# Second mixer of a two-block transformer: the recurrence's jobs, the head norms and the rotations are issued between groups of the input projection's products; the final norm becomes one DVE pass

## The chip, the cores and the metric

The kernel runs on one core of a Trainium2 chip. A core has five engines with a queue each: TensorE (PE, with its weight loads shown apart as PEld), VectorE (DVE), ScalarE (ACT), GpSimd (POOL) and SyncE (SP, which issues most DMAs). They meet only through semaphores: an engine works off its queue in order, and an instruction that waits holds everything behind it on that engine. The metric is the time of one execution of the whole program in microseconds.

## The reference, cut to what matters

A first block (two layers) makes x of 512 tokens by 1024 features. The second block is where the change is:

```python
hx = modulate(rmsnorm(x, g_norm1[l]), mx[0], mx[1])          # 512 tokens
hc = modulate(rmsnorm(ctx, g_norm1[l]), mc[0], mc[1])        # 256 context tokens
px = jnp.split(hx @ w_in[l], IN_SPLIT_IDX, axis=-1)
pc = jnp.split(hc @ w_in[l], IN_SPLIT_IDX, axis=-1)
qx = apply_rope(rmsnorm(heads(px[0], ATT_HEADS, ATT_HEAD_DIM), g_q[l]), cos, sin)
kx = apply_rope(rmsnorm(heads(px[1], ATT_KV_HEADS, ATT_HEAD_DIM), g_k[l]), cos, sin)
att_x = latent_attention(qx, kx, vx, kc, vc)
hg_x, hg_c = hgrn2_bidirectional(px[3:], pc[3:], lb_all[l], g_hg[l])
x = x + mx[2] * (jnp.concatenate([att_x, hg_x], axis=-1) @ w_out[l])
x = x + mx[5] * swiglu(...)
return rmsnorm(x, g_final)
```

`hgrn2_bidirectional` is a gated linear recurrence, four heads of 128 features, forward and backward: `fg = lb + (1 - lb) * sigmoid(f)`, the keys are `1 - fg`, the decays are `exp` of sums of `log(fg)`, and `o_t = S_t^T q_t` with `S_t = diag(fg_t) S_(t-1) + k_t v_t^T`. Its output is normed per head and multiplied by `silu(g)`.

## The kernel before, in words

Everything is kept feature-major: a tile is 128 features by 512 tokens (T) or 256 context tokens (LC). A float32 product is made of three cheaper ones: a chunk of 128 output features of a weight is loaded (`w_raw`, 4 slots), ACT copies its high half (`w_hi`, L160), DVE subtracts (`w_lo`, L166), both with 2 slots, and PE runs `w_hi*xH`, `w_hi*xL`, `w_lo*xH` for each of 8 groups of input features (L196): 24 products a chunk. Stages (`Stage` with `first_high`, `finished`, `emptied`, `high`, `low`) chain such projections.

The second mixer has four parts in a row, each a program of its own for the five queues:

1. `ProjectBoth` (L1802 to L1840): 26 chunks of `w_in`. The first 12 (attention queries, recurrence queries `hq`, output gates `hg`) multiply x alone; 14 (keys, values, `i`, forget gates `ff` and `fb`) also the 256 context columns. ACT copies each result out of its bank (L1830, L1831).
2. Head norms and rotations (L2016 to L2166): squares, means by a matrix product, `Ln` and `Exp`, rotation; six tiles. The sigmoids of all forget gates (L2024) stand here, and POOL prepares gates and keys (L2009 to L2013).
3. The attention loop, u = 0 to 31 and its tail: logits, softmax, turned probabilities, values. At u = 8 ACT takes the logarithms of all gates (`gate_logs`, L2042), and from u = 14 on DVE sums them (scans, L1923 and L1925).
4. The recurrence (L2256 to L2515). A unit u is a head and a direction (8 units). Within a block of 128 tokens the decayed products of queries and keys are made on 7 levels of halving, so there are 56 jobs n. A job is: two differences on DVE (L2415, L2416), one `Exp` on ACT (L2353), two multiplications on POOL (L2293, L2294), four products of 128x128 on PE, each of two weight loads (L2502), and a masked copy on DVE (L2404). Once a unit the decayed keys are turned (L2444, L2446), copied by ACT (L2321, L2322) and multiplied into state sums (L2455, L2458); once a head there are the diagonal (L2468), the output (L2480, L2483), its mean and its readout (L2328 to L2394).

After it the `Residual` stage begins the projection `w_out` (PE at 1854.28). At the very end the final `Norm` runs on DVE (L1289), then POOL (L1309), then SP stores (L1418).

## Time and profile before

| | us |
|---|---|
| median of 3 runs (2299.24 to 2299.47) | 2299.24 |
| the profiled execution | 2297.08 |
| its span | 2295.5 |
| PE busy in the span | 2122.0 (92%) |
| DVE busy | 1245.0 (54%) |
| ACT busy | 876.3 (38%) |
| POOL busy | 334.8 (15%) |

The mean granted TensorE clock is 0.958 of full speed. Busy times are sums over engines that run at once, so they don't add up to the span. Of the second mixer the projection ends at 1541.0, the norms and rotations at 1568.8, the attention at 1688.0, and the first product of `w_out` starts at 1854.28. Lines such as L2502 are lines of the kernel before, unless they are said to be of the changed kernel.

### The profile page before, as it was taken

The page shows a single profiled execution, that of the slowest core. Times are in us where ns is not written, and L with a number is a line of the kernel's source. Part 1 is how long each engine was busy: PE and PEld are TensorE (multiplying, and loading weights), DVE is VectorE, ACT ScalarE, POOL GpSimd, SP SyncE. Part 2 cuts the span into 40 slices and gives each one's busy share as a digit, 9 for nine tenths or more (in the row PEclk, how much of TensorE's full clock was granted, in tenths as well). Part 3 has the DMA queues.
Part 4 walks back from the last instruction along what each step waited for, and adds up shares of the span by engine and source line. Part 5 has one row for each costly group of instructions (what it writes and reads, how often), then busy time and mean ns, then how long its engine had stood idle before and what let it go on. Part 6 is the DMA issues. An engine that isn't in the chain of part 4 may idle for free. (4 is left out here: it accounts for less than half of the span.)

```text
span 2295.5 us, 27519 instructions
## 1 busy us (share of the span) xinstructions
PE 2122.0 (92%) x9734; PEld 1678.5 (73%) x9734; DVE 1245.0 (54%) x1922; ACT 876.3 (38%) x1345; POOL 334.8 (15%) x412
## 2 busy tenths in 40 slices
PE   8999879999999899899999979997877788999996
PEld 6666547888888677688888848884656667888885
DVE  3666437788667655766653352116749934333323
ACT  4433534444422443444442242227554524222222
POOL 0033312010000210100000030004039802000001
PEclk9999899999999999999999989997988889999998
DMA  5211002566445222132332212210000022333330
GB/s 190 76 44 37 1 29 67 183 197 193 151 156 157 95 83 83 56 101 92 100 116 96 81 37 92 64 46 1 1 10 10 13 79 66 101 91 101 110 101 37
DMA packets 52624, 191.78 MB, mean 84 GB/s; under 512 B 5792, under 2 KB 8512, under 8 KB 52288
## 3 DMA queue, kind: packets, MB, share of 16 engines
q1 hardware_dynamic: 44672, 163.07, 22.2%
q0 software_dynamic: 7344, 27.27, 3.8%
q8 instruction: 47, 0.77, 0.1%
q10 hardware_dynamic: 528, 0.40, 0.1%
q14 instruction: 33, 0.27, 0.0%
HBM read 187.05 MB, written 3.67 MB: 83 GB/s over the span
## 5 line engine op out<-in xcount | busy, mean ns | idle before, releaser
L196 PE MATMUL psum<-xH,w_hi 128*128 128x512 f32 x1800 | 719.0, 399 | 48.2 <-DVE xL L1297 23.5
L196 PE MATMUL psum<-xL,w_hi 128*128 128x512 f32 x1800 | 707.9, 393 | 0.0
L196 PE MATMUL psum<-xH,w_lo 128*128 128x512 f32 x1800 | 707.6, 393 | 0.0
L166 DVE TENSOR_TENSOR w_lo<-w_raw,w_hi 128x1024 fp32r<-128x1024 f32 (+1 forms) x273 | 353.4, 1295 | 443.9 <-ACT w_hi L160 443.9
L160 ACT ACTIVATE w_hi<-w_raw 128x1024 fp32r<-128x1024 f32 (+1 forms) x273 | 303.1, 1111 | 398.6 <-PE psum L196 394.1
L196 PEld LDWEIGHTS psum<-xH,w_hi 128*128 128x128 f32 x1800 | 342.0, 190 | 147.9 <-DVE xL L1297 38.4
L196 PEld LDWEIGHTS psum<-xH,w_lo 128*128 128x128 f32 x1800 | 342.1, 190 | 72.8
L196 PEld LDWEIGHTS psum<-xL,w_hi 128*128 128x128 f32 x1800 | 342.8, 190 | 67.9 <-issue 0.5
L196 PE MATMUL psum<-hidH,w_hi 128*128 128x512 f32 x528 | 206.2, 391 | 0.0
L196 PE MATMUL psum<-hidH,w_lo 128*128 128x512 f32 x528 | 205.4, 389 | 0.0
L196 PE MATMUL psum<-hidL,w_hi 128*128 128x512 f32 x528 | 205.4, 389 | 0.0
L1375 DVE SCALAR_TENSOR_TENSOR gate_value<-psum,cols,gate_value 128x511 f32<-128x511 f32 x88 | 66.0, 750 | 133.5 <-ACT gate_value L1348 132.5
L1348 ACT ACTIVATE gate_value<-psum,cols 128x512 f32<-128x512 f32 x88 | 60.7, 689 | 164.0 <-PE psum L196 164.0
L1311 POOL TENSOR_SCALAR xT<-y,cols 128x512 f32<-128x512 f32 x32 | 40.1, 1262 | 554.8 <-DVE y L1289 554.8
L196 PEld LDWEIGHTS psum<-hidH,w_hi 128*128 128x128 f32 x528 | 99.1, 188 | 21.1 <-issue 0.5
L196 PEld LDWEIGHTS psum<-hidL,w_hi 128*128 128x128 f32 x528 | 99.1, 188 | 21.0 <-issue 0.5
L196 PEld LDWEIGHTS psum<-hidH,w_lo 128*128 128x128 f32 x528 | 99.1, 188 | 20.5
L2502 PE MATMUL psum<-gla_mixed 128*128 128x128 f32 x448 | 70.7, 310 | 33.6 <-POOL gla_mixed L2294 30.7
L2502 PEld LDWEIGHTS psum<-gla_mixed 128*128 128x128 f32 x448 | 61.8, 214 | 43.1 <-POOL gla_mixed L2294 40.7
L612 ACT ACTIVATE logits<-logits,stat 128x128 f32<-128x128 f32 (+3 forms) x64 | 36.0, 562 | 107.2 <-DVE stat L740 107.1
L740 DVE CUSTOM_DVE_ANT_0 logits<-psum,addend 128x128 f32<-128x128 f32 (+3 forms) x64 | 31.3, 490 | 82.6 <-PE psum L846 80.4
L1378 DVE SCALAR_TENSOR_TENSOR gate_value<-psum,cols,gate_value 128x510 f32<-128x510 f32 x88 | 65.9, 748 | 11.1 <-DVE gate_value L1375 2.8
(312 smaller groups left out, 2538.0 us busy)
## 6 DMA issues: line engine op xcount, KB each, us to landing
w_raw<-in_up SPq DMA_DIRECT2D x132, 512.0 KB, 3.5
w_raw<-in_down SPq DMA_DIRECT2D x48, 704.0 KB, 4.0
mod_raw<-in_mod POOLq DMA_DIRECT2D x48, 512.0 KB, 3.8
w_raw<-in_sb_in SPq DMA_DIRECT2D x26, 512.0 KB, 3.5
w_raw<-in_ev_in SPq DMA_DIRECT2D x23, 512.0 KB, 3.6
w_raw<-in_od_in SPq DMA_DIRECT2D x20, 512.0 KB, 3.5
w_raw<-in_ev_out SPq DMA_DIRECT2D x8, 512.0 KB, 3.5
w_raw<-in_od_out SPq DMA_DIRECT2D x8, 512.0 KB, 3.4
```

Of the source, the lines that this page charges most:

```text
L160: nc.scalar.activation(w_hi[:, s % SPLIT, 0:w.cols], raw[:, s, 0:w.cols], ACT.Copy).then_inc(w.high, 1)
L166: nc.vector.tensor_tensor(w_lo[:, s % SPLIT, 0:w.cols], raw[:, s, 0:w.cols], w_hi[:, s % SPLIT, 0:w.cols].bitcast(F32), ALU.subtract).then ...
L196: mm = nc.tensor.matmul(acc, a[:, slot % SPLIT, cut], b[:, k0 + k, :], start=start and n == 0, stop=stop and n == 2)
L612: nc.scalar.activation(t, t, ACT.Exp, bias=stat[:, 0, s:s + 1], scale=-1.0, accum_out=stat[:, 1, s:s + 1]).then_inc(a["exp"], 1)
L740: nc.vector.tensor_tensor_reduce(out=tl[:, s % RING, 0:n], in0=logits_bank(s)[:, 0:n], in1=Xa[:, s % 3, 0:n], scale=-1.0 if kind == "a" el ...
L1311: ins = nc.gpsimd.tensor_scalar(dst, yt[:, t % 3, 0:self.n], self.gain(t), self.shift(t), ALU.mult, ALU.add)
L1348: nc.scalar.activation(value if j % 2 else gate, bank[j % 2][:, :], ACT.Copy, scale=self.tap(i, j, 2)).then_inc(ff["tap"], 1)
L1375: nc.vector.scalar_tensor_tensor(y[:, 1:T], acc[:, 0:T - 1], self.tap(i, j, 1), y[:, 1:T], ALU.mult, ALU.add).then_inc(ff["conv"], 1)
L1378: self.emptied(nc.vector.scalar_tensor_tensor(y[:, 2:T], acc[:, 0:T - 2], self.tap(i, j, 0), y[:, 2:T], ALU.mult, ALU.add), j)
L2502: mm = nc.tensor.matmul(bank[n % 3][:, blk(c)], x[:, blk(c)], x[:, blk(c)], start=True, stop=True)
```

## The change

`ProjectBoth`, the head norms, the attention and the recurrence become one stage, `SecondMixer`. The chunks of `w_in` come in a new order, `SB_LIST`: forget gates and `i` head by head, then keys, values, queries and output gates. From the third chunk on the products are cut into 76 `PARTS` of 12 products: two parts of 512 columns, and for a chunk with context two of 256 columns. After part p PE does job p - 14 of the recurrence, DVE and ACT do their share of job p - 11 at their own part p; POOL goes job by job. `sigmoid`, POOL's `gates`, `gate_logs` and `sum_gates` are done for one head at a time, between jobs. All turned tiles of the recurrence use one bank (5), each turn waiting until the one before has been copied out (`turned_out`). The context products use bank 2 alone. Head means and rotations run at p = 61 to 71. The attention loop keeps ten steps of the recurrence's readout. The first two chunks are not interrupted. The final norm is one `scalar_tensor_tensor` on DVE, in place, and the stores wait for it.

```diff
+                        if self.kind == "final":
+                            y = self.x[:, t, :]
+                            nc.vector.scalar_tensor_tensor(y, y, self.gain(t), rstd[:, :], ALU.mult, ALU.mult).then_inc(nm["y"], 1)
+                            continue
...
+                if self.kind == "final":
+                    return
...
-                    sp.wait_ge(nm["affine"], self.norm.at("affine", t))
-                    sp.dma_start(out[:, t, :], ht[:, t % 3, :]).then_inc(s_out[t % 3], 16)
-                for s in range(3):
-                    sp.wait_ge(s_out[s], 16 * len(range(s, KD, 3)))
+                    sp.wait_ge(nm["y"], self.norm.at("y", t))
+                    sp.dma_start(out[:, t, :], self.norm.x[:, t, :]).then_inc(s_out, 16)
+                sp.wait_ge(s_out, 16 * KD)
```

The order of the chunks, the parts and the offsets:

```diff
+        SB_LIST = [("hq", 0), ("hq", 1), ("ff", 0), ("fb", 0), ("i", 0), ("ff", 1), ("fb", 1), ("i", 1),
+                   ("hq", 2), ("ff", 2), ("fb", 2), ("i", 2), ("hq", 3), ("ff", 3), ("fb", 3), ("i", 3),
+                   ("k", 0), ("v", 0), *(("q", m) for m in range(4)), *(("hg", m) for m in range(HG))]
+        PLACE = {"hq": SB_HQ, "ff": SB_FF, "fb": SB_FB, "i": SB_I, "k": SB_K, "v": SB_V, "q": SB_Q, "hg": SB_HG}
+        W["sb_in"].order = tuple(PLACE[name] + m for name, m in SB_LIST)
...
+        PARTS, FIRST = [], {}
+        for c, (name, _) in enumerate(SB_LIST):
+            FIRST[c] = len(PARTS)
+            if c >= SPLIT:
+                PARTS += [(c, False, 0), (c, False, 4)] + ([(c, True, 0), (c, True, 4)] if name in C_TILE else [])
+        ENDED = {FIRST[c + 1] if c + 1 < SB_N else len(PARTS): c for c in range(1, SB_N)}
...
+        AHEAD = 11
+        PE_AT = 14
```

POOL (gates of one head, decayed keys, the loop) and ACT (results, sigmoids, logarithms, the keys' copy, the loop):

```diff
+                def gates(hd):
+                    pool.wait_ge(g["sig"], 4 * hd + 5)
+                    for d in range(2):
+                        u, t = 2 * hd + d, d * HG + hd
                         for f in (bx(u), bc(u)):
                             nc.gpsimd.tensor_scalar(f, f, lbs[:, 5, t:t + 1], lbs[:, 0, t:t + 1], ALU.mult, ALU.add)\
                                 .then_inc(g["fg"], 1)
...
+                def to_end(u):
+                    pool.wait_ge(g["to_end"], u + 1)
+                    x0 = (u % 2) * P
+                    nc.gpsimd.tensor_tensor(kds[:, 0:3 * P], kds[:, 0:3 * P], kx[:, u % 4, x0:x0 + 3 * P], ALU.mult)
+                    nc.gpsimd.tensor_tensor(kds[:, 3 * P:5 * P], kds[:, 3 * P:5 * P], kc[u % 4][:, :], ALU.mult).then_inc(g["kd"], 1)
...
+                gates(0)
+                for n in range(JOBS):
+                    u, l = n // LEVELS, n % LEVELS
+                    pool.wait_ge(g["exp"], n + 1)
+                    if n >= 3:
+                        pool.wait_ge(g["level"], n - 2)
+                    eq, ek, _ = halves(dec[:, n % 4, :], u, l)
+                    mq, mk, _ = halves(mixed[:, n % 3, :], u, l)
+                    nc.gpsimd.tensor_tensor(mq, halves(hq(u // 2), u, l)[0], eq, ALU.mult)
+                    nc.gpsimd.tensor_tensor(mk, halves(kx[:, u % 4, :], u, l)[1], ek, ALU.mult).then_inc(g["mult"], 1)
+                    if l == 2:
+                        to_end(u)
+                    hd = due(n, 9, 2 * LEVELS, HG - 1)
+                    if hd is not None:
+                        gates(hd + 1)
...
+                def result(c):
+                    name, m = SB_LIST[c]
+                    self.finished(act, 0, c)
+                    if c in CTX_DONE:
+                        nc.scalar.activation(sb_hc[:, C_TILE[name](m), :], bank[2][:, 0:LC], ACT.Copy).then_inc(ctx_out, 1)
+                    if name == "hg":
+                        act.wait_ge(g["mult"], JOBS)
+                    self.emptied(nc.scalar.activation(sb_hT[:, X_TILE[name](m), :], bank[c % 2][:, :],
+                                                      ACT.Silu if c < SPLIT else ACT.Copy), c)
+                    self.high(act, 0, c, c + SPLIT < w.n)
+
+                def sigmoid(hd):
...
+                    for u in (2 * hd, 2 * hd + 1):
+                        for f in (bx(u), bc(u)):
+                            nc.scalar.activation(f, f, ACT.Sigmoid).then_inc(g["sig"], 1)
+
+                def gate_logs(hd):
+                    act.wait_ge(g["k"], 4 * hd + 4)
+                    for u in (2 * hd, 2 * hd + 1):
+                        for f in (bx(u), bc(u)):
+                            nc.scalar.activation(f, f, ACT.Ln).then_inc(g["ln"], 1)
...
+                def kd_out(u, half):
+                    act.wait_ge(g["turned"], kd_turn_no(u, half))
+                    if half == 0 and u:
+                        act.wait_ge(g["kv"], u)
+                    dst = kd_tm[:, 0:3, :] if half == 0 else kd_tm[:, 3:5, :]
+                    src = bank[5][:, 0:(3 - half) * P].rearrange("t (c k) -> t c k", c=3 - half)
+                    nc.scalar.activation(dst, src, ACT.Copy).then_inc(g["turned_out"], 1)
...
+                def decays(n):
+                    if 0 <= n < JOBS:
+                        act.wait_ge(g["diff"], n + 1)
+                        d = dec[:, n % 4, :]
+                        nc.scalar.activation(d, d, ACT.Exp).then_inc(g["exp"], 1)
...
+                result(0)
+                for p in range(len(PARTS)):
+                    if p in ENDED:
+                        result(ENDED[p])
+                    hd = due(p, 20, 14, HG - 1)
+                    if p == 8 or hd is not None:
+                        sigmoid(0 if p == 8 else hd + 1)
+                    hd = due(p, 23, 14, HG - 1)
+                    if p == 11 or hd is not None:
+                        gate_logs(0 if p == 11 else hd + 1)
+                    decays(p - AHEAD)
```

DVE and PE:

```diff
+                def sum_gates(hd):
+                    dve.wait_ge(g["ln"], 4 * hd + 4)
+                    dve.wait_ge(g["inside"], 2)
+                    for u in (2 * hd, 2 * hd + 1):
+                        turn = slice(None, None, 1 if u % 2 == 0 else -1)
+                        nc.vector.tensor_tensor_scan(bx(u)[:, turn], inside[:, :], bx(u)[:, turn], 0.0, ALU.mult, ALU.add)\
+                            .then_inc(g["scan"], 1)
+                        nc.vector.tensor_tensor_scan(bc(u)[:, turn], bc(u)[:, turn], bc(u)[:, turn], 0.0, ALU.add, ALU.bypass)\
+                            .then_inc(g["scan"], 1)
...
+                def difference(n):
+                    u, l = n // LEVELS, n % LEVELS
...
+                    nc.vector.tensor_tensor(dq, q, border, ALU.subtract)
+                    nc.vector.tensor_tensor(dk, border, k, ALU.subtract).then_inc(g["diff"], 1)
...
+                def gla(n):
+                    hd = due(n, -1, 2 * LEVELS, HG)
+                    if hd is not None:
+                        sum_gates(hd)
+                    if 0 <= n < JOBS:
+                        difference(n)
+                    u = due(n, 10, LEVELS, U7)
+                    if u is not None:
+                        states(u)
+                    if 3 <= n < JOBS + 3:
+                        select(n - 3)
...
+                def part(c, ctx, k0):
+                    if k0 == 0 and not ctx:
+                        pe.wait_ge(acc_free[c % 2], self.free_at(0, c))
+                        pe.wait_ge(w.low, w.c0 + c + 1)
+                    elif k0 == 0 and CTX_DONE[c] > 1:
+                        pe.wait_ge(ctx_out, CTX_DONE[c] - 1)
+                    right = (cH, cL) if ctx else self.right
+                    acc = bank[2][:, 0:LC] if ctx else bank[c % 2][:, :]
+                    for k in range(k0, k0 + 4):
+                        mm = product(pe, w, c, right, acc, k, 0, k == 0, k == KD - 1)
+                    if k0 and (ctx or c not in CTX_DONE):
+                        mm.then_inc(w.used, 1)
+
+                def level(n):
+                    pe.wait_ge(g["mult"], n + 1)
+                    if n >= 2:
+                        pe.wait_ge(g["pred"], n - 1)
+                    x = mixed[:, n % 3, :]
+                    for c in range(NB):
+                        mm = nc.tensor.matmul(bank[3 + n % 2][:, blk(c)], x[:, blk(c)], x[:, blk(c)], start=True, stop=True)
+                    mm.then_inc(g["level"], 1)
...
+                def turn_keys(u, half):
+                    pe.wait_ge(g["kd"], u + 1)
+                    pe.wait_ge(g["turned_out"], kd_turn_no(u, half) - 1)
+                    for c in range(3 - half):
+                        mm = nc.tensor.transpose(bank[5][:, blk(c)], kds[:, blk(3 * half + c)], ident[:, :])
+                    mm.then_inc(g["turned"], 1)
...
+                def gla(n):
+                    if 0 <= n < JOBS:
+                        level(n)
+                        u, l = n // LEVELS, n % LEVELS
+                        if l < 2 and u % 2 == 0:
+                            turn_values(u // 2, l)
+                        if l in (2, 3):
+                            turn_keys(u, l - 2)
+                        if l == 5:
+                            sums(u)
...
+                for p, (c, ctx, k0) in enumerate(PARTS):
+                    part(c, ctx, k0)
+                    gla(p - PE_AT)
```

The order of instructions, first on PE in the recurrence. Before, the level products of consecutive jobs (L2502) stand directly behind one another, with the key turns (L2444, L2446) between them:

```order
L2502 MATMUL psum<-gla_mixed 128x128 [waits gla_pred,gla_mult]
L2502 MATMUL psum<-gla_mixed 128x128 x3
L2444 MATMUL psum<-ident,sb_hT 128x128 [waits gla_kd_out,gla_kd]
L2444 MATMUL psum<-ident,sb_hT 128x128 x2
L2446 MATMUL psum<-ident,sb_hT 128x128 x2
L2502 MATMUL psum<-gla_mixed 128x128 [waits gla_pred,gla_mult]
```

After, at the part that ends in job 10 (unit 1, the second half of its key turn; L2432 is the level product and L2449 the key turn of the changed kernel, L196 a product of the projection):

```order
L196 MATMUL psum<-xH,w_lo 128x512
L2432 MATMUL psum<-gla_mixed 128x128 [waits gla_pred,gla_mult]
L2432 MATMUL psum<-gla_mixed 128x128 x3
L2449 MATMUL psum<-ident,gla_keys_decayed 128x128 [waits gla_turned_out,gla_kd]
L2449 MATMUL psum<-ident,gla_keys_decayed 128x128
L196 MATMUL psum<-xH,w_hi 128x512
```

The turn of the keys now has projection products ahead of it and behind it, and it waits for `gla_turned_out`, the copy of its first half by ACT.

On ACT, before, that copy (L2321) stands behind a decay's `Exp` and the `Exp`s of one unit:

```order
L2309 ACTIVATE sb_hT<-sb_hT 128x128 [waits gla_kd_turned]
L2309 ACTIVATE sb_hT<-sb_hT 128x128 x2
L2310 ACTIVATE sb_hT<-sb_hc 128x256
L2315 ACTIVATE sb_hT<-sb_hT 128x512 [waits gla_state,gla_qe]
L2353 ACTIVATE gla_decay<-gla_decay 128x512 [waits gla_diff]
L2321 ACTIVATE gla_kd_tm<-psum 128x384 [waits gla_kv,gla_kd_turned]
```

After, the copy for unit 1 (L2109) at ACT's part 24, and what stands ahead of it: the logarithms of the next head (L2087), which wait for POOL's gates, a result (L2066, L2069), a high half (L160) and decays (L2145):

```order
L2087 ACT_TABLE_LOAD
L2087 ACTIVATE sb_hT<-sb_hT 128x512 [waits gla_k]
L2087 ACTIVATE sb_hc<-sb_hc 128x256
L2087 ACTIVATE sb_hT<-sb_hT 128x512
L2087 ACTIVATE sb_hc<-sb_hc 128x256
L2145 ACT_TABLE_LOAD
L2145 ACTIVATE sb_hT<-sb_hT 128x512 [waits gla_diff]
L2066 ACTIVATE sb_hc<-psum 128x256 [waits w_used]
L2069 ACTIVATE sb_hT<-psum 128x512
L160 ACTIVATE w_hi<-w_raw 128x1024 [waits w_used,w_loaded1]
L2145 ACTIVATE sb_hT<-sb_hT 128x512 [waits gla_diff]
L2109 ACTIVATE gla_kd_tm<-psum 128x384 [waits gla_kv,gla_turned]
```

The logarithms moved from the attention loop to a place ahead of the copy.

On DVE, after, at its part 24: the scans of the next head (L2265, L2267) between a low half (L166) and the differences (L2278, L2279) for which the last `Exp` above waits; before, all scans stood in the attention loop.

```order
L166 TENSOR_TENSOR w_lo<-w_raw,w_hi 128x1024 [waits w_high]
L2265 SCALAR_TENSOR_TENSOR sb_hT<-gla_inside,sb_hT 128x512 [waits gla_inside,gla_ln]
L2267 SCALAR_TENSOR_TENSOR sb_hc<-sb_hc 128x256
L2265 SCALAR_TENSOR_TENSOR sb_hT<-gla_inside,sb_hT 128x512
L2267 SCALAR_TENSOR_TENSOR sb_hc<-sb_hc 128x256
L2278 TENSOR_TENSOR sb_hT<-sb_hT 128x256 [waits gla_mult]
L2279 TENSOR_TENSOR sb_hT<-sb_hT 128x256
```

The scans now have jobs ahead of them and behind them.

## Rows read from the trace of the kernel before

**Rows 1.** Windows of the four parts: start:end and length, then busy us (instructions).
```profile
core 0: us, PE busy (x) PEld busy (x) DVE busy (x) ACT busy (x) POOL busy (x), PEclk, DMA share, GB/s
1369.30:1541.00 171.70, 171.70 (x915) 148.67 (x913) 28.30 (x24) 39.73 (x60) 0.00 (x0) 1.00 0.21 68
1541.00:1568.80 27.80, 18.84 (x53) 10.26 (x52) 19.08 (x30) 23.76 (x33) 6.97 (x7) 0.79 0.10 33
1568.80:1688.00 119.20, 101.65 (x512) 70.72 (x512) 74.33 (x132) 73.36 (x131) 22.06 (x32) 0.89 0.00 1
1688.00:1854.30 166.30, 115.27 (x730) 102.47 (x729) 132.27 (x223) 82.42 (x153) 121.45 (x132) 0.82 0.04 13
```
**Rows 2.** Waits in the recurrence, 1690 to 1850: us, times, longest.
```profile
PEld psum L2502 <- POOL gla_mixed L2294: 40.7, 40, 2.5
```
**Rows 3.** Instruction groups of the recurrence, 1700 to 1840: busy us, mean ns, idle before.
```profile
L2502 PE MATMUL psum<-gla_mixed 128*128 128x128 f32 x448 | 70.7, 310 | 33.6 <-POOL gla_mixed L2294 30.7 <-DVE gla_weights L2404 2.8
L2294 POOL TENSOR_TENSOR gla_mixed<-gla_k,gla_decay 128x256 f32<-128x256 f32 x56 | 54.8, 979 | 0.0
L2293 POOL TENSOR_TENSOR gla_mixed<-sb_hT,gla_decay 128x256 f32<-128x256 f32 x56 | 49.2, 878 | 13.0 <-ACT gla_decay L2353 12.8
L2404 DVE COPY_PREDICATED gla_weights<-gla_masks,psum 128x512 f32<-128x512 uint8 x56 | 40.8, 729 | 15.2 <-PE psum L2502 14.9
L2353 ACT ACTIVATE gla_decay<-gla_decay 128x512 f32<-128x512 f32 x56 | 34.5, 625 | 52.3 <-DVE gla_decay L2416 52.3
```
**Rows 4.** Timeline of PE's weight loads in the recurrence: start us, us.
```profile
1711.60 0.97 PEld L2502 LDWEIGHTS psum<-gla_mixed 128*128 128x128 f32 x8 [1.74 <-POOL gla_mixed L2294]
```
**Rows 5.** Timeline of PE in an earlier projection, a mean product between products.
```profile
1226.05 1.02 PE L1106 MATMUL psum<-xT,mean_of 128*128 128x512 f32 x2
...
1227.14 0.40 PE L196 MATMUL psum<-hidL,w_hi 128*128 128x512 f32 x1
1227.38 0.40 PE L196 MATMUL psum<-hidH,w_lo 128*128 128x512 f32 x1
```
**Rows 6.** Instruction groups on ACT and DVE in the projection, 1369.3 to 1541.
```profile
L160 ACT ACTIVATE w_hi<-w_raw 128x1024 fp32r<-128x1024 f32 x23 | 24.3, 1057 | 0.0
L166 DVE TENSOR_TENSOR w_lo<-w_raw,w_hi 128x1024 fp32r<-128x1024 f32 x24 | 29.4, 1226 | 132.8 <-ACT w_hi L160 132.8
L1831 ACT ACTIVATE sb_hT<-psum 128x512 f32 x23 | 13.7, 595 | 40.8 <-PE psum L196 40.8
L1830 ACT ACTIVATE sb_hc<-psum 128x256 f32 x12 | 4.6, 385 | 78.5 <-PE psum L196 78.5
```
**Rows 7.** Timeline of POOL: the gates of one unit start, those of the next.
```profile
1590.66 0.77 POOL L2009 TENSOR_SCALAR sb_hT<-sb_hT,gla_lb 128x512 f32<-128x512 f32 x1
...
1593.05 0.77 POOL L2009 TENSOR_SCALAR sb_hT<-sb_hT,gla_lb 128x512 f32<-128x512 f32 x1
```
**Rows 8.** Instruction groups of the scans on DVE, 1541 to 1690.
```profile
L1923 DVE TENSOR_TENSOR_SCAN sb_hT<-gla_inside,sb_hT 128x512 f32<-128x512 f32 x8 | 9.7, 1217 | 0.0
L1925 DVE TENSOR_TENSOR_SCAN sb_hc<-sb_hc 128x256 f32<-128x256 f32 x8 | 5.5, 683 | 0.0
```
**Rows 9.** Timeline of DVE at the first difference of the recurrence.
```profile
1690.18 0.42 DVE L2415 TENSOR_TENSOR gla_decay<-sb_hT 128x256 f32<-128x256 f32 x1 [0.32 <-PEq L1984]
```
**Rows 10.** Timeline of ACT around the gates' logarithms.
```profile
1591.24 0.60 ACT L2053 ACTIVATE probs_t<-psum 128x512 f32<-128x512 f32 x1
1591.85 1.28 ACT L2042 ACT_TABLE_LOAD   x1
1593.15 1.91 ACT L2042 ACTIVATE sb_hT<-sb_hT 128x2048 f32<-128x2048 f32 x1
...
1600.07 0.90 ACT L2068 ACTIVATE probs<-psum,stat 128x768 f32<-128x768 f32 x1
```
**Rows 11.** Timeline of PE at the first products after the recurrence.
```profile
1854.28 0.76 PE L196 MATMUL psum<-xH,w_hi 128*128 128x512 f32 x1 [8.47 <-DVE w_lo L166]
...
1857.40 0.39 PE L196 MATMUL psum<-xL,w_hi 128*128 128x512 f32 x1
```
**Rows 12.** Timeline of the final norm.
```profile
2282.92 1.90 DVE L1289 TENSOR_TENSOR y<-xT,rstd 128x512 f32<-128x512 f32 x3 [4.89 <-ACT rstd L1261]
2283.71 8.27 POOL L1309 TENSOR_SCALAR h<-y,cols 128x512 f32<-128x512 f32 x7 [362.05 <-DVE y L1289]
2285.33 0.69 DVE L1289 TENSOR_TENSOR y<-xT,rstd 128x512 f32<-128x512 f32 x1 [0.51 <-POOL h L1309]
2292.30 0.69 POOL L1309 TENSOR_SCALAR h<-y,cols 128x512 f32<-128x512 f32 x1 [0.31 <-DMA out<-h]
```

More of the change, by code:

```diff
@@ L1282, in vector @@
                     if t < KD:
-                        if t >= 3:
+                        if t >= 3 and self.kind != "final":
                             dve.wait_ge(nm["affine"], self.at("affine", t - 3))
@@ L1792, in build @@
+        gain_hg, at = sb("gla_gain", [P, 1], at=at)
+        assert at <= split_end
+        rope, at = sb("rope", [P, 4, T], at=CTX_AT)
+        nrot, at = sb("head_rot", [P, 2, T], at=at)
+        nsin, at = sb("head_sin", [P, 2, T], at=at)
+        qst, at = [], CTX_AT
+        for n in range(2):
+            tile, at = sb(f"queries_split{n}", [P, 4, T], F32R, at=at)
+            qst.append(tile)
         NK = LC + T
         KT = NK // P
[L1794 removed]
```

918 lines of the change are left out of this document (425 added, 493 removed).

## The prediction

> **What bounds the kernel now.** I read the windows of the second mixer first [rows 1]. While the projection runs, PE is busy all 171.7 us at full clock, with DVE busy 28, ACT 40 and POOL not at all. The three parts behind it last 27.8 + 119.2 + 166.3 = 313.3 us, and there PE has 18.8, 101.7 and 115.3 us of work and a granted clock of 0.79, 0.89 and 0.82. The recurrence is the one to look at. The waits say that PE's weight loads stood 40.7 us for POOL's product [rows 2], and the groups show POOL with 54.8 + 49.2 us for the 56 jobs and hardly an idle moment [rows 3]: a job costs POOL 1.86 us, so POOL sets the pace. The change puts POOL's work beside products that need no POOL. What can be won is therefore large, what it costs is PE time and new waits, and the sum is about which of them is larger.
>
> **PE work added to the products.** A job's eight weight loads take 0.97 us at full clock [rows 4], 0.121 each. The mixed part has 448 loads for the 56 jobs, 80 for state sums, 40 for key turns, 24 for value turns, 32 for diagonals, 96 for outputs and 6 for turned attention values, 726 in all: 88.0 us. A float32 mean of 512 columns between products costs 1227.14 - 1226.05 less one product step of 0.23, so 0.86 [rows 5]; three head means of the recurrence are 2.6, and ten such tiles of head norms and rotations with one of half the width 9.0. Together **99.6 us**. Two bounded additions: a job took PE 1.26 us before (70.7 / 56, [rows 3]) against 0.97 of loads, so each of some 80 changes of kind costs between 0 and 0.3, 0 to 24 in all; I take 5, since the next product's load runs under the last multiplication. After a wait, PE runs at half speed: eight products from 1854.28 to 1857.40 took 3.1 us where the full-speed step gives 1.6 [rows 11]. Five long waits below cost 1.6 each, 8 us. So 13 more.
>
> **New waits of PE.** A product of 512 columns takes a step of 0.23 (1227.38 less 1227.14, [rows 5]), one of 256 about 0.12: the projection's window with its 579 and 336 of them is 171.7 long, which gives 0.228 and 0.12. A chunk with context is 24 x 0.228 + 24 x 0.12 = 8.36 us of PE, its parts 2.74 (512 columns) and 1.44.
>
> The wait that the order shows: PE's second key turn of unit 1 (part 24) needs the copy of the first half, which ACT has at its own part 24 behind the logarithms of the next head, a result and a high half. Queued behind that turn on PE are the products themselves. The chain from part 20, when PE has just finished the chunk of the backward gates:
> - ACT: starts 1.0 late; copies 0.38 + 0.60 and high half 1.06 [rows 6]; table 1.28; four sigmoids 2.0 (two of 0.6, two of 0.4); table 1.28, an Exp 0.63 [rows 3, 10]
> - POOL: the multiplications of job 9, 1.86, its decayed keys about 1.9 (two such operations), the gates of two units, 2 x 2.39 (1593.05 - 1590.66) = 4.8 [rows 3, 7]
> - ACT: four logarithms 2.0 (their table load lies in the wait), table 1.28, Exp 0.63, result and high half 2.07
> - DVE: low half 1.23 [rows 6], scans 2 x (1.217 + 0.683) = 3.8 [rows 8], two differences 0.84 (0.42 each with POOL idle, [rows 9])
> - ACT: Exp 0.63 and the copy 0.5.
>
> Sum 29.8 us. PE has in the meantime 8.36 + 2.74 + five jobs 4.85 + turns 0.6 = 16.5. It waits 13.3. For heads 2 and 3 (parts 38 and 52) the chain has also a Silu with its table, 1.91, and an output's copies, 1.2, and PE a mean, 0.86: 15.5 each. **44.3 us** for the three. This rests on how the queues are ordered, since every piece has its own row.
>
> The first head has the same chain at part 8, now up to job 3: results and high halves 2.0 + 2.0, table and sigmoids 3.3, gates 4.8, tables 2.6, logarithms 2.0, scans 3.8, difference 0.84, two Exps 1.3, the first unit's five Exps 2.3, one more 0.6, three times POOL's 1.86 to 1.9: 31.2, with 2.7 for the late start and what DVE interposes (a low half, a select) 33.9. PE's work to there is 22.2 of products and 4.0 of jobs and turns: **7.7 us**. At parts 30 and 44 a low half comes late by about 1.5 each, **3**. At parts 60 to 75 mean, copy, gain, turn and sine of a head go through bank 2 in a ring. At a chunk's start the ring has a result 0.6, a high half 1.06, an Exp 0.63, a square 0.63, a copy 0.6, a gain 0.64, a low half 1.23 and a select 0.73, 6.1 us, where PE has a part and a job, 3.7: five times 2.4, and 2.5 for the value turns, **14.7**. All waits: 69.7.
>
> **What the three parts behind become.** From the products' end to the first logits: the last result, key and query halves, seven or eight operations of about 0.6, 4.6 us. The attention loop keeps 119.2, loses ACT's logarithms (from 1591.85 to 1600.05, 8.2 us in which the next exponent was due, [rows 10]), and gains one Silu of 2048 columns with two table loads, 1.28 + 1.91 + 1.28, and the last head's readout, 5 together: 116.0. DVE's scans leave it as well, but DVE was busy only 74 of 119 us. Before `w_out`: the last attention halves 0.6 + 0.7, then w_hi 1.06, w_lo 1.23 and 0.5 to enter, 4.1; before, 8.5 us of readout stood there too.
>
> **Sum** from 1541.0 on: 99.6 + 69.7 + 13 + 4.6 + 116.0 + 4.1 = 307.0 against 313.3: -6.3 us.
>
> **The final norm.** Before, DVE starts at 2282.92, POOL works from 2283.71 with 1.18 a tile and ends at 2292.99 [rows 12]: POOL is the pace, not DVE (0.69 a tile). One pass with two factors isn't in the trace at this place; I bound it by the 0.69 of the plain product and POOL's 1.18, and take 0.72, as its form reads two tiles like the product. Eight of them end at 2288.7: -4.3 us, with 0 if it took 1.2.
>
> Together -10.6: the profiled execution's 2297.08 would become 2286.5, and the median, 2.2 above it, 2299.24 - 10.6 = 2288.6, **2289**. A measurement here tells apart about 0.2%, 4.6 us: faster is below 2294.6, slower above 2303.8.
>
> **Rivals.**
> - *The waits don't come about; PE sets the pace.* Per 14 jobs PE has 53 us of work, DVE about 44, ACT 40, POOL 37: no engine but PE is full on the average. If queues drift so that the late chain meets slack elsewhere, all 69.7 us go: 2219; if half do, 2254. Against it: at part 24 PE waits for a copy that is ordered behind a chain longer than its own work, and slack elsewhere doesn't shorten a chain. For it: my chain adds each piece end to end, and eight of its pieces might overlap. 0.25.
> - *Slower: the clock.* The granted clock was 1.00 only where PE never waited, and 0.82 and 0.89 in the two parts where it waited in short pieces [rows 1]. The mixed part has 171.7 + 99.6 = 271 us of PE work with a wait every 60 us and small ones between. If it gets 0.89, that work takes 33.5 us longer in place of the 8 that I gave, 2289 + 25 = 2314. No change to the median is reached when the loss grows from 8 to 18.6 us, a mean clock of 0.936. For it: the projection's own window had no such waits. Against it: between the waits PE is full for tens of microseconds, and after 1857.40 it is at full speed again. 0.20.
> - *Table switches are dearer.* In the trace a load starts 0.01 us after the operation before it has ended, and the next operation 0.02 after the load, 1591.84 to 1593.15 [rows 10]: 1.28 us for a switch. If each switch on the chains cost as much again, 1.28, while the engine empties, thirteen of them (three on each of the four heads' chains, one at the Silu) make +17: 2306. Against it stand the two gaps of 0.02 and less. 0.05.
>
> The Trainium skill, page "ScalarE: Activation LUTs", section "What ACT_TABLE_LOAD costs", gives for a switch a drain of about 1.4 us on top of the load; by its figure the last rival would be an estimated 2307. The rows above don't show the drain.
>
> **How the numbers follow.** My forecast, waits of some 70 us give or take 12, has 0.50 and a range of its own of 2276 to 2302: 0.32 of it below 2294.6, 0.13 within, 0.05 above 2303.8. The first rival adds 0.25 faster, the clock 0.20 slower (0.02 of which ends within), the tables 0.05, half within. Faster 0.57, same 0.17, slower 0.26. The likely range reaches down to the half case, 2252, and up to the clock case, 2316; outside lie the fuller part of the first rival, 0.12, and the tail of the second, 0.05.
>
> **What would show it.** In the profile after: from about 1370 to the first logits some 354 us in one window, with POOL busy some 130 of them; PE waits of 13 to 16 us at key turns at three places some 53 us apart, released by ACT's copy of the decayed keys, with POOL's gates and DVE's scans in the time before; a wait of 8 us at the first head's; no waits of level products for POOL beyond those; a POOL without instructions after 2280; a last store about 4 us earlier against the last rstd. I'm wrong if the three waits are under 5 us (then the time is below 2265), if the mixed window's clock is below 0.94, or if a low half stops PE at chunk after chunk, which would mean that ACT or DVE is late all along, not at four places. The sizes are least sure in the ring of the head norms, where 14.7 could be 5 or 25.

## The result and the profile after

The changed kernel takes 2271.5 us (median of 4 runs, 2268.55 to 2274.16) against 2299.24; the ratio is 0.9884, with a 95% interval from 0.9872 to 0.9895. It is 27.7 us faster, where I had forecast 10.6. The sign, the place of the longest waits and the final norm came out as written; the size of the gain did not.

The windows of the mixed stage, cut at its main waits, then the step to the first logits, the attention and the entry of `w_out` (columns as in [rows 1]):

```profile
core 0: us, PE busy (x) PEld busy (x) DVE busy (x) ACT busy (x) POOL busy (x), PEclk, DMA share, GB/s
1353.90:1402.90 49.00, 48.37 (x224) 38.77 (x224) 19.66 (x34) 20.50 (x29) 17.13 (x18) 0.89 0.20 65
1402.90:1465.00 62.10, 44.25 (x262) 39.05 (x262) 33.48 (x55) 30.90 (x57) 32.17 (x41) 0.84 0.11 35
1465.00:1534.00 69.00, 55.00 (x354) 49.17 (x353) 38.29 (x61) 37.09 (x63) 34.27 (x41) 0.90 0.10 31
1534.00:1603.00 69.00, 54.97 (x346) 48.98 (x346) 38.36 (x61) 36.59 (x62) 34.29 (x41) 0.88 0.09 31
1603.00:1709.50 106.50, 94.92 (x535) 78.67 (x534) 59.16 (x90) 48.64 (x83) 36.23 (x37) 1.00 0.15 50
1709.50:1713.60 4.10, 0.96 (x3) 0.13 (x1) 2.54 (x4) 3.86 (x6) 0.00 (x0) 0.93 0.00 0
1713.60:1826.70 113.10, 95.99 (x512) 67.34 (x512) 62.90 (x117) 71.27 (x135) 0.00 (x0) 0.93 0.00 1
1826.70:1830.80 4.10, 0.00 (x0) 0.00 (x0) 2.03 (x3) 2.59 (x3) 0.00 (x0) 0.79 0.00 0
```

From the first product of `w_in` (1353.98) to the first of `w_out` (1830.84) it is 476.9 us. Before it was 501.0 (1353.28 to 1854.28), so this stretch gave 24.1 of the 26.3 us between the two spans. I had given it 6.3. The granted clock over the whole mixed part (1353.9 to 1709.5) is 0.91. Next, PE's waits from 1360 to 1710 (us, times, longest):

```profile
PE psum L2449 <- ACT gla_kd_tm L2109: 23.8, 5, 7.2
PE psum L2432 <- POOL gla_mixed L2044: 13.8, 4, 4.2
PE psum L2442 <- ACT gla_v_tm L2117: 9.4, 4, 3.5
PE psum L2520 <- DVE head_sin L2330: 4.4, 4, 1.9
PE psum L2525 <- ACT sb_hT L2172: 2.1, 1, 2.1
PE psum L196 <- ACT sb_hc L2066: 1.6, 1, 1.6
PE psum L2542 <- DVE values L2353: 1.3, 1, 1.3
```

With some pieces below 1 us they make 57.6 us. The first row is the wait that the forecast named: the second key turn for ACT's copy, at three head boundaries 69 us apart (I had written 53, which is PE's own work between them and leaves the wait out). How one of them arises is read on three engines. PE, at the level product of job 10 and the turn behind it:

```profile
1443.17 0.55 PE L2449 MATMUL psum<-ident,gla_keys_decayed 128*128 128x128 f32 x3
1450.56 2.08 PE L2432 MATMUL psum<-gla_mixed 128*128 128x128 f32 x8 [4.07 <-POOL gla_mixed L2044]
1459.82 0.66 PE L2449 MATMUL psum<-ident,gla_keys_decayed 128*128 128x128 f32 x2 [7.18 <-ACT gla_kd_tm L2109]
```

ACT (L2081 a sigmoid's table, L2087 the logarithms, L2109 the copy):

```profile
1434.25 1.28 ACT L2081 ACT_TABLE_LOAD   x1
1435.54 0.63 ACT L2081 ACTIVATE sb_hT<-sb_hT 128x512 f32<-128x512 f32 x1
...
1447.84 0.63 ACT L2087 ACTIVATE sb_hT<-sb_hT 128x512 f32<-128x512 f32 x1 [4.51 <-POOL gla_kc L2015]
1448.38 0.40 ACT L2087 ACTIVATE sb_hc<-sb_hc 128x256 f32<-128x256 f32 x1
...
1452.19 1.06 ACT L160 ACTIVATE w_hi<-w_raw 128x1024 fp32r<-128x1024 f32 x1
1458.66 0.63 ACT L2145 ACTIVATE sb_hT<-sb_hT 128x512 f32<-128x512 f32 x1 [5.41 <-DVE sb_hT L2279]
1459.20 0.47 ACT L2109 ACTIVATE gla_kd_tm<-psum 128x384 f32<-128x384 f32 x1
```

And DVE between them, the low half and the first scan:

```profile
1453.28 1.28 DVE L166 TENSOR_TENSOR w_lo<-w_raw,w_hi 128x1024 fp32r<-128x1024 f32 x1 [9.23 <-ACT w_hi L160]
1454.49 1.21 DVE L2265 TENSOR_TENSOR_SCAN sb_hT<-gla_inside,sb_hT 128x512 f32<-128x512 f32 x1
```

The copy at 1459.20 was ready to be made since PE's first half at 1443.17. It stood behind four logarithms (which waited 4.5 us for POOL's gates), a high half, and an `Exp` that waited for the scans. PE waited twice on the same chain, 4.07 us at the level product that POOL owed it and 7.18 us at the turn: 11.25 us, where I had put 13.3 at the one place. A wait of a level product for POOL was one that I had said would not come.

The final norm, which answers to [rows 12]:

```profile
2261.24 5.39 DVE L1289 SCALAR_TENSOR_TENSOR xT<-xT,cols,rstd 128x512 f32<-128x512 f32 x8 [3.94 <-ACT rstd L1261]
```

Eight passes of 0.67 us. From their start to the end of the span it is 8.0 us, before 12.6: 4.6 less, forecast 4.3.

### The profile page after: what moved, and what is told of

It is laid out like the page before. It is cut to its first block and busy times, and to the rows that moved or that the text cites. A ratio compares the mean times of both kernels' runs of the same rounds, so it can differ in the third digit from the quotient of the medians.

```text
span 2269.2 us, 27321 instructions
## 1 busy us (share of the span) xinstructions
PE 2097.4 (92%) x9710; PEld 1660.5 (73%) x9710; DVE 1239.7 (55%) x1922; ACT 902.1 (40%) x1396; POOL 317.0 (14%) x404
## 5 line engine op out<-in xcount | busy, mean ns | idle before, releaser
L196 PE MATMUL psum<-xH,w_hi 128*128 128x512 f32 x1800 | 731.0, 406 | 42.8 <-DVE xL L1301 22.7
L196 PE MATMUL psum<-xL,w_hi 128*128 128x512 f32 x1800 | 713.1, 396 | 0.0
L196 PE MATMUL psum<-xH,w_lo 128*128 128x512 f32 x1800 | 712.7, 396 | 0.0
L166 DVE TENSOR_TENSOR w_lo<-w_raw,w_hi 128x1024 fp32r<-128x1024 f32 (+1 forms) x273 | 355.5, 1303 | 381.4 <-ACT w_hi L160 381.3
L160 ACT ACTIVATE w_hi<-w_raw 128x1024 fp32r<-128x1024 f32 (+1 forms) x273 | 303.1, 1111 | 399.7 <-PE psum L196 395.2
L196 PEld LDWEIGHTS psum<-xH,w_hi 128*128 128x128 f32 x1800 | 345.1, 192 | 144.2 <-DVE xL L1301 37.9
L196 PEld LDWEIGHTS psum<-xH,w_lo 128*128 128x128 f32 x1800 | 345.0, 192 | 74.5
L196 PEld LDWEIGHTS psum<-xL,w_hi 128*128 128x128 f32 x1800 | 345.5, 192 | 71.2 <-issue 3.1
L196 PE MATMUL psum<-hidH,w_hi 128*128 128x512 f32 x528 | 206.2, 391 | 0.0
L196 PE MATMUL psum<-hidH,w_lo 128*128 128x512 f32 x528 | 205.4, 389 | 0.0
L196 PE MATMUL psum<-hidL,w_hi 128*128 128x512 f32 x528 | 205.4, 389 | 0.0
L196 PEld LDWEIGHTS psum<-hidH,w_hi 128*128 128x128 f32 x528 | 99.1, 188 | 21.0 <-issue 0.5
L196 PEld LDWEIGHTS psum<-hidL,w_hi 128*128 128x128 f32 x528 | 99.1, 188 | 20.9 <-issue 0.5
L196 PEld LDWEIGHTS psum<-hidH,w_lo 128*128 128x128 f32 x528 | 99.1, 188 | 20.7
L2301 DVE COPY_PREDICATED gla_weights<-gla_masks,psum 128x512 f32<-128x512 uint8 x56 | 41.3, 738 | 76.9 <-PE psum L2432 75.2
L2145 ACT ACTIVATE sb_hT<-sb_hT 128x512 f32<-128x512 f32 x56 | 34.9, 629 | 112.4 <-DVE sb_hT L2279 112.3
L2432 PE MATMUL psum<-gla_mixed 128*128 128x128 f32 x448 | 62.3, 284 | 13.8 <-POOL gla_mixed L2044 13.8
```

The lines of the kernel that those rows point to most:

```text
L160: nc.scalar.activation(w_hi[:, s % SPLIT, 0:w.cols], raw[:, s, 0:w.cols], ACT.Copy).then_inc(w.high, 1)
L166: nc.vector.tensor_tensor(w_lo[:, s % SPLIT, 0:w.cols], raw[:, s, 0:w.cols], w_hi[:, s % SPLIT, 0:w.cols].bitcast(F32), ALU.subtract).then ...
L196: mm = nc.tensor.matmul(acc, a[:, slot % SPLIT, cut], b[:, k0 + k, :], start=start and n == 0, stop=stop and n == 2)
L2145: nc.scalar.activation(d, d, ACT.Exp).then_inc(g["exp"], 1)
L2301: nc.vector.copy_predicated(aT[:, hd % 2, :, :], level_mask[d][:, l * P:(l + 1) * P].unsqueeze(1).to_broadcast([P, NB, P]), bank[3 + n % 2 ...
L2432: mm = nc.tensor.matmul(bank[3 + n % 2][:, blk(c)], x[:, blk(c)], x[:, blk(c)], start=True, stop=True)
```

## The experiments

My theory after the result: the gain was cut by waits of PE, and these are copies and products queued on ACT, POOL and DVE behind the preparation of the next head; the forecast gave the chains right in place and too long in sum. The first rival: PE's own work and clock set the stage, and the waits would only move. The second: the difference lies outside the mixed stage (attention, final norm). A median carries with it the scatter of the rest of the program; a table behind the runs gives, from each trace, the length of the part in which the edits lie. The kernel before, run again beside each group of experiments, had medians of 2297.45 to 2298.86 us.

**The final norm put back.** The kernel of this run is the changed one with the final norm's code of before, its three slots on semaphores that are free by then.

```diff
-                            nc.vector.scalar_tensor_tensor(y, y, self.gain(t), rstd[:, :], ALU.mult, ALU.mult).then_inc(nm["y"], 1)
+                        ins = nc.gpsimd.tensor_scalar(dst, yt[:, t % 3, :], self.gain(t), 1.0, ALU.mult, ALU.mult)
```

> The changed kernel with the final norm of before (DVE, POOL, three slots), all else as changed. Its tail from the first DVE pass to the end of the span took 8.0 us after and 12.6 before. If the final norm is worth what the trace shows, this kernel is 4.6 us slower than the changed one (about 2276) and the second mixer is as in the changed one. Rival: the stores hide the difference, then within 1 us of the changed kernel.

2277.92 us (2276.59 to 2278.69), 0.9909 of the kernel before (0.9892 to 0.9925). The first DVE pass starts at 2263.85 and the span ends at 2276.4: 12.55 us again, 4.6 more than in the changed kernel. The medians differ by 6.4 us; the two intervals, each some 3 us to either side, leave room for 4.6. The norm is worth 4.6 and isn't where the forecast went wrong.

**The scans of heads 1 to 3 left out.**

```diff
+                        if hd:
+                            nc.vector.tensor_copy(bx(u)[:, 0:1], bx(u)[:, 0:1]).then_inc(g["scan"], 2)
+                            continue
```

> Leaves out the four scans of heads 1 to 3 (a one-column copy stands in for them). Chain theory: PE's second key turn of units 1, 3 and 5 waits 7.2 us at the end of one chain through ACT, POOL and DVE, in which two scans of each kind are 3.4 us; without them each wait is 3.4 us shorter, 10 us in all (about 2261), the POOL wait of 4.1 before it stays. Rival (something else ends that wait, ACT's tables or the chunk's low half, which stands ahead of the scans): the waits shrink by less than 1 us each and the time stays within 3 us.

2260.51 us (2259.62 to 2261.5), 11.0 less than the changed kernel (forecast 10). PE's waits for the copy went from 23.8 to 14.4, the waits for POOL stayed:

```profile
PE psum L2452 <- ACT gla_kd_tm L2109: 14.4, 5, 4.4
PE psum L2435 <- POOL gla_mixed L2044: 13.8, 4, 4.2
```

At the three heads the wait got 3.3, 3.3 and 2.8 us shorter, where the scans left out were 3.3 of DVE's time. So DVE's scans, which run on an engine that is busy little over half the time, are on the path of PE almost microsecond for microsecond.

**The keys' copy one part earlier.**

```diff
-                        u = due(n, 6 + half, LEVELS, U7)
+                    for half in range(2):
+                        u = due(n, 5 + half, LEVELS, U7)
```

> ACT copies the turned keys one part earlier (5 + half in place of 6 + half), ahead of the result, the high half and the Exp that waits for the scans. Nothing is left out. Chain theory: the 7.2 us waits at the three second key turns vanish, since the copy no longer stands behind the scans, and what the scans delay next, the level product of the head's last job two parts later, has slack: 15 to 21 us less, about 2252, with the POOL wait of 4.1 us left. Rival (the wait only moves to the level product or to the next low half): less than 5 us gained.

2251.63 us (2246.68 to 2253.13), 19.9 less than the changed kernel, 0.9792 of the kernel before (0.9775 to 0.9808), and within the forecast of 15 to 21. ACT now copies behind the logarithms and one `Exp`, before the result and the high half, and PE's turn follows its level product with no wait. ACT and then PE in this kernel:

```profile
1453.23 0.47 ACT L2109 ACTIVATE gla_kd_tm<-psum 128x384 f32<-128x384 f32 x1
1453.60 0.38 ACT L2066 ACTIVATE sb_hc<-psum 128x256 f32<-128x256 f32 x1
```
```profile
1452.35 1.67 PE L2433 MATMUL psum<-gla_mixed 128*128 128x128 f32 x8 [4.08 <-POOL gla_mixed L2044]
1453.85 0.66 PE L2450 MATMUL psum<-ident,gla_keys_decayed 128*128 128x128 f32 x2
```

All three waits of 7.2 us are gone and nothing like them took their place: PE waits 37.9 us in the mixed part, 19.7 less, with 2.8 more in two rows of the ring of the head norms and 1.2 for one select. A place in ACT's order, not work, had cost 0.9% of the kernel.

**POOL's gates ahead of job 9.** POOL calls `gates(hd + 1)` before that job's products in place of behind them.

> POOL prepares the next head's gates before the products of job 9 and the decayed keys of unit 1, not behind them. Nothing is left out. Chain theory: the chain up to the copy gets 3.8 us shorter (1.75 and 2.07 of POOL, less what now waits at the first key turn), the 4.1 us wait of the level product moves to the key turn: 2 to 4 us less a head, 6 to 12 in all, about 2262. Rival (POOL's order doesn't matter, ACT's table loads and Exps set the chain): within 3 us.

2266.34 us (2264.53 to 2267.57), 5.2 less, just under the 6 to 12 of the theory and outside the 3 of the rival. PE's waits for the copy fell by 4.2 to 19.6 and those for POOL by 2.7 to 11.1. POOL's order is on the chain, with a smaller share than I had given it, since what is put behind the gates is itself waited for: PE's key turn now has a wait for POOL's decayed keys, 1.0 us in two pieces.

**Both.**

> Both edits of the two runs before: keys copied one part earlier, and POOL's gates ahead of job 9's products. If the gates' place mattered only through the chain to the copy (which is now gone), it adds nothing: the wait of 4.1 us stays, at another level product, and the time is that of the early copy alone, 2251, or up to 3 us slower. Rival (the two add up): 2246 or less.

2244.83 us (2244.57 to 2248.34), 6.8 less than the early copy alone. That is the rival's figure. My condition for it was wrong: the gates' place works without the chain to the copy too, for PE's wait for POOL is 10.9 here and 13.8 there. By the stage's length (457.1 and 451.8 us) the gain is 5.3, but 1.6 of that lies in the attention loop, where the edit does nothing; up to the first logits it is 3.7, close to the 4.4 that the gates' place gave alone.

**The turned values' copies earlier as well.**

```diff
-                        hd = due(n, 4 + half, 2 * LEVELS, HG)
+                        hd = due(n, 3 + half, 2 * LEVELS, HG)
```

> Keys' copies one part earlier, and the turned values' copies too (3 + half in place of 4 + half). Theory: the waits of 2.2 us a head and of 3.5 us at the first head stand behind the same pattern, a copy out of the single bank queued behind an Exp on ACT, and vanish: 8 to 10 us less than the early key copy alone, about 2242. Rival (ACT reaches the copy no earlier, since it then waits for PE): less than 3 us less.

2240.22 us (2235.92 to 2241.12), 11.4 less than the early key copy alone (forecast 8 to 10). The waits of 2.2 us a head are gone, that of the first head went from 3.5 to 0.9.

**POOL's preparation in three pieces.**

```diff
+                    for part in range(3):
+                        hd = due(n, 9 + part, 2 * LEVELS, HG - 1)
+                        if hd is not None:
+                            if part < 2:
+                                gates(2 * hd + 2 + part)
+                            else:
+                                key_sum(hd + 1)
```

> As the run before, and POOL's preparation for a head is cut into three (first unit after job 9, second after job 10, the keys' sum after job 11). Theory: the three waits of 4.1 us of the level product for POOL, which are the whole preparation (4.7 and 1.3 us) less the slack, go to below 1 us: another 9 to 12 us less, about 2231, PE waits in the mixed part then below 20. Rival (the logarithms come later with the second unit's gates and the scans then hold up a low half): 5 us or less.

2242.18 us (2238.69 to 2245.11): nothing gained, and in the trace the mixed part is 4.0 us longer. The waits for POOL fell to 0.6 at each head, and a wait for the copy is back:

```profile
1448.23 0.66 PE L2456 MATMUL psum<-ident,gla_keys_decayed 128*128 128x128 f32 x2 [5.43 <-ACT gla_kd_tm L2115]
```

The early copy stands behind the logarithms on ACT, and these now wait for POOL's second piece. The rival was right that the wait moves, though not in where it goes.

**The logarithms and scans later.**

```diff
-                    hd = due(p, 23, 14, HG - 1)
-                    if p == 11 or hd is not None:
-                        gate_logs(0 if p == 11 else hd + 1)
+                    if p == 11:
+                        gate_logs(0)
                     decays(p - AHEAD)
+                    hd = due(p, 24, 14, HG - 1)
+                    if hd is not None:
+                        gate_logs(hd + 1)
```

> As the run with the gates split in three, which put a wait of 5.4 us at the second key turn in place of the 4.1 us at the level product, since the early copy on ACT stood behind the logarithms, and these behind POOL's second unit. Here the logarithms of heads 1 to 3 come after job 13's Exp and the copies on ACT, and the scans after job 13's difference and select on DVE. Theory: nothing that PE needs within three parts stands behind the logarithms any more, so both waits are below 1 us at each of the three heads: 12 us less than the early copies alone, about 2229. Rival (the wait moves again, to the next low half or to the first level product of the new head): 2236 or more.

2231.77 us (2227.41 to 2233.86), 8.5 less than with the early copies, between the two figures. The waits for the copy are down to two of 0.5 us. The waits for POOL are 8.4 us in nine pieces of 1.6 at most. Of the 7.0 us by which the mixed part got shorter only 3.7 are waits; the other 3.3 are PE's own work, done at a granted clock of 1.00 from 1414 to 1575, where the kernel with the early copies and its three waits of 4.1 us had 0.96 from 1414 to 1580.

**The sine product first,** in the kernel above and alone in the changed kernel:

```diff
+                    if p - 1 in TURNS:
+                        head_rope(TURNS[p - 1])
                     gla(p - AHEAD)
-                    if p - 1 in TURNS:
-                        head_rope(TURNS[p - 1])
```

> As the run before, and DVE makes the sine product of a head ahead of the job's differences and select. Ring theory: the waits of 1.9, 1.8, 0.8 and 1.5 us of the next mean for that product are what stands ahead of it on DVE (2.1 us), so they go: 5 us less, about 2224. Rival (the ring's period is that of the copies on ACT): less than 2 us.

> The changed kernel with only the sine product moved ahead of the job on DVE. Ring theory: 5 us less than the changed kernel, about 2266, its waits for the sine gone from the trace. Rival: within 2 us.

2225.58 us (2224.69 to 2226.87), 6.2 less, and alone 2264.6 us (2263.57 to 2268.37), 6.9 less. In both the waits for `head_sin` are gone from the trace, 6.0 us of them in the kernel above and 4.4 in the changed kernel; by the mixed part's length the edit is worth 6.9 and 4.2, so some of the 6.9 between the medians of the second pair is scatter. The ring was paced in good part by what stood ahead of the product on DVE.

The traces of all these kernels, from the first product of `w_in` to the first logits (mixed part) and from there to the end of the last attention product, in us:

| kernel | mixed part | attention |
|---|---|---|
| changed | 359.7 | 113.0 |
| norm put back | 360.1 | 113.0 |
| no scans | 351.7 | 114.6 |
| keys' copy early | 338.4 | 114.6 |
| gates first | 355.3 | 114.6 |
| both | 334.7 | 113.0 |
| both kinds of copies early | 326.2 | 113.0 |
| gates in three pieces | 330.1 | 114.6 |
| logarithms late | 319.2 | 113.0 |
| sine product first | 312.3 | 113.0 |
| sine product first, alone | 355.5 | 114.5 |

No edit changes the attention loop, yet it takes one of two lengths 1.6 us apart. What sets it I have not traced.

The best version is 3.1% below the kernel before (ratio 0.9688, 0.9675 to 0.9702) and 45.9 us below the changed one. It differs from the latter only in the order of instructions and in the waits that go with it. In a window at the same times, first the changed kernel, then this one, whose PE gets through more instructions in it:

```profile
1412.00:1603.00 191.00, 148.53 (x913) 131.97 (x914) 105.13 (x167) 98.30 (x167) 96.56 (x118) 0.87 0.10 31
```
```profile
1412.00:1603.00 191.00, 179.55 (x1181) 159.13 (x1182) 135.40 (x206) 117.96 (x209) 126.94 (x142) 1.00 0.14 45
```

**The attention before, without the scans.**

> The kernel before; leaves out the sixteen scans (one-column copies stand in) and takes the gates' logarithms of a constant. The attention window was 119.2 us. I forecast 116.0 after and it came out at 113.0. If the 3 us are the scans' share of the loop, it is about 116 here; rival (DVE's scans were hidden, and the logarithms alone had cost more than their 8.2 us): 119 here.

One profiled execution. First logits and last products of the attention:

```profile
1567.17 0.55 PE L2179 MATMUL psum<-keys_split,xH 128*128 128x256 f32 x1 [2.89 <-DVE xH L1963]
...
1677.66 5.39 PE L2202 MATMUL psum<-probs_t,values 128*64 128x256 f32 x24
```

From 1567.17 to 1683.05 it is 115.9 us, 3.3 less than the 119.2 of before. That is what the scans' share was to be (about 116), and not the rival's 119. It is one trace against one, and the loop of the changed kernels scatters by 1.6 us, so the scans had very likely not been hidden; by that scatter I estimate their price at 2 to 5 us.

## Why the forecast was off

The step that failed is the size of the new waits. The mechanism held: PE work added to the products, and waits of PE at the head boundaries behind one chain through ACT, POOL and DVE. But I gave the three head boundaries 44.3 us where the trace has 33.9, and the ring of the head norms 14.7 where it has 9.2; the attention loop and PE's own work came out 3.0 and 2.4 us shorter too, and only the other waits were longer, by 5.0. Most terms erred to the same side.

The working from 1541.0 on gave 307.0 us; the trace gives 476.9 less the 187.7 that the products took before, 289.2. Term by term, forecast and measured; PE's work is what is left of 289.2 when the other rows are taken off:

| term | forecast | measured |
|---|---|---|
| PE work added, changes of kind, half speed | 112.6 | 110.2 |
| wait at the first head | 7.7 | 6.5 |
| the three head boundaries | 44.3 | 33.9 |
| other waits between jobs | 3.0 | 8.0 |
| the ring of the head norms | 14.7 | 9.2 |
| products' end to first logits | 4.6 | 4.2 |
| attention | 116.0 | 113.0 |
| entry of `w_out` | 4.1 | 4.2 |

*What bounds the kernel, and that POOL's work would lie beside products*: right. POOL is busy 154 us in the stage and PE waits 13.8 for it.

*PE work added*: right, 2% high. That the weight loads give the price of a job held: eight take 1.05 us with their multiplications, and stand 3.6 us apart with a part of products (2.74) between, so a job adds 0.9 us where I had 0.97.

*The waits at the heads*: this step failed in size. At the first boundary, from the start of part 20 on PE (1430.90) to the second key turn (1459.82), it is 28.9 us where I had 29.8, and PE's own work in it is 17.7 where I had 16.5, since the level product behind the first wait took 2.08 us and not 1.05. So 11.3 us of wait, not 13.3. Within the chain two errors partly cancel: ACT's first copy came 1.5 us after PE's start and not 1.0, and from it (1432.44) to the turn it is 27.4 us where my durations sum to 28.8. Neighbours on ACT overlap: the logarithms start at 1447.84 and 1448.38, 0.54 apart for 0.63. The same goes for DVE's scans (1.21 us, next 1.13 later). For the second and third I lengthened the chain by 3.1 us, for a Silu and an output's copies, and that is where most of the error lies. ACT and PE at the second:

```profile
1499.28 0.37 ACT L2066 ACTIVATE sb_hc<-psum 128x256 f32<-128x256 f32 x1
1517.11 0.63 ACT L2087 ACTIVATE sb_hT<-sb_hT 128x512 f32<-128x512 f32 x1 [2.78 <-POOL gla_kc L2015]
```
```profile
1519.83 2.08 PE L2432 MATMUL psum<-gla_mixed 128*128 128x128 f32 x8 [4.17 <-POOL gla_mixed L2044]
1529.08 0.66 PE L2449 MATMUL psum<-ident,gla_keys_decayed 128*128 128x128 f32 x2 [7.17 <-ACT gla_kd_tm L2109]
```

From the start of part 34 on PE (1499.50) to the turn it is 29.6 us where I had 32.9, and PE's own work is 18.2 where I had 17.4. The chain is only 0.7 us longer than at the first boundary: ACT's first copy came 0.2 us ahead of PE's start and not 1.5 behind it, and ACT waited 2.78 us in place of 4.51 for POOL, so part of the added work ran in time in which it would have been idle. A cause was thus right at all three, and its size 2 us too large at one and 4 at two.

*The first head*: 6.5 for 7.7, but not as one wait. It is 1.6 for a context copy, 1.4 for POOL and 3.5 for the copy of the turned values, which my chain didn't have. That the sum is near is in part luck.

*The ring of the head norms*: the 6.1 us put everything of ACT and DVE in a row (and my pieces sum to 14.5, not 14.7). The sine product ahead of the job removed waits of 4.4 of the 9.2 us, so DVE's part was there. Which of ACT's pieces ran beside it no run separates.

*Other waits*: under-forecast by 5. The low halves that I had late at parts 30 and 44 were not late. What stood there instead I had not seen: the turned values share bank 5, and their copies have the place on ACT that the keys' have; I had costed only the keys'. Moving both copies is what showed it.

*The attention*: "DVE's scans leave it as well, but DVE was busy only 74 of 119 us" was the sentence that failed. Busy share is no measure of cover in a loop whose steps wait for each other; the run without scans put their price at 3.3 us, and I was off by 3.0. Up to 1.6 us of either can be the loop's own scatter, so that the two agree so well is in part luck.

*The rivals and the signs*: that all waits vanish did not come about by itself, but 39 of the 57.6 us could be had by order alone, and the time then is near that rival's figures (2219 for none, 2254 for half). Of my three signs of being wrong one came true: the mixed part's clock was to be 0.94 or more and is 0.91. (The waits at the three turns, announced as 13 to 16 us, are 7.2, above the 5 that I had set as the sign, and no low half stopped PE chunk after chunk.) The clock fell as its rival said, to 0.84 to 0.90 over the three head boundaries, and yet it did not cost what the rival said. From the wait at 1402.98 to that at 1584.43 there are 147.0 us of work between 34.4 of waits; in the best version the same work takes 142.1 with 8.2 of waits at a clock of 1.00. Had all that work run at the 0.87 that the profile gives for those windows together, it would have taken some 163 us. It took 4.9 more than 142.1, so the low mean belongs mostly to the time in which PE waited. Over the whole mixed part PE's work is 302.1 us and 293.5 in the best version, so the loss is some 9, and my 8 for it was about right. Table loads took 1.28 us with no drain that shows: the load at 1434.25 is followed by its sigmoid at 1435.54, so nothing of that rival shows.

The sum is a difference of two numbers near 300 us. An error of 6% in one of them, most of its terms erring high, is the 18 us between 6 and 24. A margin of 12 us on the waits alone was too narrow for that: the waits came out 12.1 lower, and the other terms erred the same way.

Of the 26.3 us between the spans 24.1 lie in this stretch and 4.6 in the norm; the rest of the program was 2.4 us longer in this one execution. Since the starts of this stage vary by 6 us among the traces of kernels that are alike up to there, I take that for scatter and have not traced it.

## What to carry to other kernels

When work of several queues is woven into a stream of products, read each engine's order at the place where most new work meets, and ask of every instruction that PE waits for what stands ahead of it; a copy one place later can cost more than the work it carries. Moving such an instruction adds no work, and the profile's list of waits says which; but the wait may only move, as it did when POOL's preparation was cut in three. Here the moves together gave 45.9 us, more than the 27.7 of the change itself. A chain forecast by adding mean durations counts overlaps twice and leaves out idle time that can take up new work; where a forecast is a small difference of large sums, widen it by some per cent of the sums.

## What the runs showed of the hardware

The same multiplication on POOL took less time while DVE was idle. In the changed kernel, with DVE idle from 1444 to 1453:

```profile
1449.12 0.71 POOL L2043 TENSOR_TENSOR gla_mixed<-sb_hT 128x256 f32<-128x256 f32 x1
1449.80 0.71 POOL L2044 TENSOR_TENSOR gla_mixed<-gla_k,sb_hT 128x256 f32<-128x256 f32 x1
```

The mean over the recurrence before was 0.88 and 0.98 [rows 3]. DVE's difference shows the other side, 0.41 us alone and 0.94 at 1442.46 beside POOL. The Trainium skill, page "SBUF — State Buffer", section "SBUF: two separate sides", says that a DVE operation with two inputs in SBUF and a GpSimd operation that reads SBUF take a shared port pair in turn and not in halves; the rows agree with that in direction, and no run here separates it from other causes.

The granted clock is low behind PE's long waits. The level product behind the wait of 4.07 us took 2.08 us for eight loads and multiplications, the same one without a wait 1.05:

```profile
1437.37 1.05 PE L2432 MATMUL psum<-gla_mixed 128*128 128x128 f32 x8
1450.56 2.08 PE L2432 MATMUL psum<-gla_mixed 128*128 128x128 f32 x8 [4.07 <-POOL gla_mixed L2044]
```

Long waits so cost more than their length, and the clock over the three head boundaries rose from 0.87 to 1.00 when they went and only waits of 1.6 us and less were left.
